# Handing a block's output to the next block by halves of the tokens, at five seams

## The reference

```python
def rmsnorm(x, g):
    xf = x.astype(jnp.float32)
    y = xf * lax.rsqrt(jnp.mean(xf * xf, axis=-1, keepdims=True) + NORM_EPS)
    return y.astype(x.dtype) * g
...
    for l in range(DEPTH):
        g = norm_gains[l]
        h = rmsnorm(x, g[0])
        ...
        x = x + rmsnorm(y, g[1])
        h = rmsnorm(x, g[2])
        x = x + rmsnorm(memory_cross_attention(h, mem_n, w_mem_q[l], w_mem_kv[l], w_mem_o[l]), g[3])
        h = rmsnorm(x, g[4])
        x = x + rmsnorm(squared_relu_mlp(h, w_ff1[l], w_ff2[l]), g[5])
```

## Time and profile before

| | us |
|---|---|
| median of 3 runs | 3533.23 |
| lowest, highest | 3530.51, 3547.64 |
| the profiled execution, its own time | 3536.43 |
| its span in the trace | 3535.1 |
| PE busy | 3241.8 (92%) |
| DVE, ACT, POOL busy | 2233.2, 1430.9, 1710.6 |

### The profile page before, as it was taken

One profiled execution on the slowest core, in us unless ns is written; L12 is line 12 of the kernel. 1 busy time (PEld: TensorE's weight loads), 2 busy tenths in 40 slices (PEclk: granted clock), 3 DMA queues, 4 the chain that ended last, 5 costly groups with the idle time before them and its releaser, 6 DMA issues.

```text
span 3535.1 us, 48085 instructions
## 1 busy us (share of the span) xinstructions
PE 3241.8 (92%) x18529; PEld 2735.6 (77%) x18529; DVE 2233.2 (63%) x3780; ACT 1430.9 (40%) x2264; POOL 1710.6 (48%) x931
## 2 busy tenths in 40 slices
PE   5997888999999888999798898999999998999997
PEld 5876676888777666888576755799999998788885
DVE  4176556555644546532567646266998995877887
ACT  4454444222434444233353424433333674333333
POOL 5742323444432313444332201447888544888884
PEclk9997999999999999999898999999999999999998
DMA  5520213444332212432221011347899898999995
GB/s 190 182 75 24 84 40 98 150 140 140 102 99 80 83 35 90 151 119 96 81 72 43 2 37 60 108 144 278 297 323 325 270 311 300 372 364 351 351 354 197
DMA packets 304819, 584.76 MB, mean 165 GB/s; under 512 B 13520, under 2 KB 224464, under 8 KB 287312
## 3 DMA queue, kind: packets, MB, share of 16 engines
q1 hardware_dynamic: 252512, 373.32, 31.2%
q0 software_dynamic: 42576, 153.83, 12.2%
q10 hardware_dynamic: 9504, 54.53, 4.0%
HBM read 522.91 MB, written 58.72 MB: 165 GB/s over the span
## 4 chain that ended last, share of the span: by engine, by line
PE 70%; DVE 9%; POOL 9%; issue 7%; ACT 4%; DMA 1%; POOLq 0%; DVEq 0%; ACTq 0%
PE bank L474 16%; PE bank L476 16%; PE bank L475 16%; POOL split_low L460 6%; PE twin L474 3%; PE twin L476 3%; PE twin L475 3%; PE bank L2858 2%; PE bank L555 2%; PE bank L2284 2%; POOL rows_arena L3224 1%; DVE branch L598 1%; PE bank L2091 1%; POOL rows_h L3224 1%; DVE residual L648 1%
## 5 line engine op out<-in xcount | busy, mean ns | idle before, releaser
L460 POOL TENSOR_TENSOR split_low<-weights,split_high 128x1024 fp32r<-128x1024 f32 x554 | 1357.1, 2456 | 1524.3 <-ACT split_high L452 1517.0
L474 PE MATMUL bank<-normed_high,split_high 128*128 128x512 f32 (+1 forms) x2032 | 751.4, 370 | 51.6 <-issue 31.0
L475 PE MATMUL bank<-normed_low,split_high 128*128 128x512 f32 (+1 forms) x2032 | 740.1, 364 | 0.0
L476 PE MATMUL bank<-normed_high,split_low 128*128 128x512 f32 (+1 forms) x2032 | 740.0, 364 | 0.0
L452 ACT CAST split_high<-weights 128x1024 fp32r<-128x1024 f32 x554 | 571.2, 1046 | 361.3 <-PE bank L476 207.1
L474 PEld LDWEIGHTS bank<-normed_high,split_high 128*128 128x128 f32 x2032 | 385.9, 190 | 101.5 <-issue 49.7
L475 PEld LDWEIGHTS bank<-normed_low,split_high 128*128 128x128 f32 x2032 | 385.9, 190 | 41.7 <-issue 2.3
L476 PEld LDWEIGHTS bank<-normed_high,split_low 128*128 128x128 f32 x2032 | 384.9, 189 | 41.5
L474 PE MATMUL bank<-split_high,wide_hidden_high 128*128 128x512 f32 x768 | 301.0, 392 | 12.6 <-DVE wide_hidden_low L3080 6.5
L475 PE MATMUL bank<-split_low,wide_hidden_high 128*128 128x512 f32 x768 | 300.0, 391 | 0.0
L476 PE MATMUL bank<-split_high,wide_hidden_low 128*128 128x512 f32 x768 | 299.8, 390 | 0.0
(11 more groups left out here) (648 smaller groups left out, 6304.3 us busy)
## 6 DMA issues: line engine op xcount, KB each, us to landing
weights<-in_w_ff SPq DMA_DIRECT2D x64, 1024.0 KB
weights<-in_peer_u SPq DMA_DIRECT2D x64, 1024.0 KB
weights<-in_peer_v SPq DMA_DIRECT2D x64, 1024.0 KB
weights<-in_cond_w SPq DMA_DIRECT2D x24, 1024.0 KB
early_table<-branch SPq DMA_DIRECT2D x128, 192.0 KB
gate_table<-arena SPq DMA_DIRECT2D x12, 2048.0 KB, 10.0
lates<-early_table ACTq DMA_DIRECT2D x32, 768.0 KB
gates<-gate_table ACTq DMA_DIRECT2D x32, 768.0 KB
```

The lines of the kernel that those rows point to most:

```text
L460: pool.do.tensor_tensor(lo, raw_unit(u), hi.bitcast(F32), ALU.subtract).then_inc(*pool.sig("split_low", u))
L474: pe.do.matmul(o, ah, bh, start=first, stop=False)
L475: pe.do.matmul(o, ah, bl, start=False, stop=False)
L476: return pe.do.matmul(o, al, bh, start=False, stop=last)
```

## The change

At each of the five seams, what is done for 512 tokens becomes twice the same for 256 tokens, and the work of the first half is put between that of the second.

- PE: where `whole_of` says 4 (the seams behind E, mem0, odd and mem1), products c = 0 to 3 stay whole, then c = 4 to 7 are made for tokens 0 to 255, then c = 4 to 7 for tokens 256 to 511. Behind mlp0 all eight go by halves. The first half's square sum stands behind the first product of the second half. Then `pe_first_halves` makes the next stage's three products for the first half of all eight operand tiles, and then for the second half.
- ACT (`act_handover`): squares, root, high operands and the next stage's weight splits in one fixed order; the first root behind the first square of the second half, and the second root behind the last square and seven (behind mlp0: six) of the first half's eight operands. The dummy Ln of `act_warm` is no longer issued at these seams.
- DVE (`dve_handover`): copies and sums, with (1, 2, 2, 0) steps of the first half's addition between them ((0, 0, 1, 0, 1, 0, 1, 0) behind mlp0).
- POOL's instructions are the same; the splits that they follow have moved on ACT: the next stage's first four units are all split during the second half's products.

The core of the diff:

```diff
+        def pe_product_halves(stage, ids, c_first, rhs, ready, emptied):
+
+            per = chunks[ids[0]].width // P
+            for t, cols_t in enumerate(HALVES):
+                for c in range(c_first, CT):
+                    ck, key = chunks[ids[c // per]], (stage, c) + half_key(t)
+                    u, cols = weights(ck, c % per)
+                    bank, empty = banks.take("product", *key)
+                    pe.wait_ge(empty, split_ready(u))
+                    for a in range(ck.n_k):
+                        pe.wait_ge(ready(a))
+                        last = triple(bank[:, 0:T // 2], [w_[:, a, cols] for w_ in unit_tiles(u)],
+                                      [r[:, cols_t] for r in rhs(a)], a == 0, a == ck.n_k - 1)
+                    last.then_inc(*pe.sig("product", *key))
+                    banks.give(("product",) + key, *emptied(c, t))
+                    used[u] = ("product",) + key
+                    yield c, t
...
+        def pe_first_halves(stage, ids, ready, emptied):
+
+            for t, cols_t in enumerate(HALVES):
+                for a in range(CT):
+                    pe.wait_ge(ready(a, t))
+                    for c in range(FIRST):
+                        u, cols = weights(chunks[ids[c // 2]], c % 2)
+                        if t == 0 and a == 0:
+                            _, empty = banks.take("product", stage, c)
+                            pe.wait_ge(empty, split_ready(u))
+                        last = triple(banks.tile("product", stage, c)[:, cols_t], [w_[:, a, cols] for w_ in unit_tiles(u)],
+                                      [r[:, cols_t] for r in h_tile(a)], a == 0, a == CT - 1)
+                        if t == 1 and a == CT - 1:
+                            last.then_inc(*pe.sig("product", stage, c))
+                            banks.give(("product", stage, c), *emptied(c))
+                            used[u] = ("product", stage, c)
...
+        def pe_close_halves(branch, halves):
+
+            for c, t in halves:
+                if t == 1 and c == whole_of(branch):
+                    pe_half_sum(branch, 0)
+            pe_half_sum(branch, 1)
+
+        def pe_half_sum(branch, t):
+            norm, key = half_post(branch, t), ("square", branch + "+") + part(branch, CT - 1, t)
+            pe_sum(norm, T // 2, 0, 2, mean, dve_tmp.tile("post_sum", branch)[:, HALVES[t]],
+                   at("post_sum", branch, *part(branch, CT - 2, t)), [("root_log", norm)])
+            pe_sum(norm, T // 2, 1, 2, mean, act_tmp.tile(*key)[:, 0:T // 2], at(*key), [("root_log", norm)])
...
+        def act_half_root(branch, t):
+            if t == 0:
+                _, empty = act_tmp.take("post_root", branch)
+                act.wait_ge(empty)
+            act_root(half_post(branch, t), 1, NORM_EPS, act_tmp.tile("post_root", branch)[:, HALVES[t]], T // 2)
+            if t == 1:
+                act_tmp.give(("post_root", branch), ("y_scaled", branch, CT - 1))
...
+        def act_handover(branch, stage, gain, ids, first):
+
+            whole = whole_of(branch)
+            for c in range(whole):
+                act_split(2 * ids[0] + c + AHEAD)
+                act_half_square(branch, c, None)
+            act_split(2 * ids[-1] + 1)
+            for c in range(whole, CT):
+                act_half_square(branch, c, 0)
+            highs = iter(range(CT))
+            for i, c in enumerate(range(whole, CT)):
+                act_half_square(branch, c, 1)
+                if i == 0:
+                    act_half_root(branch, 0)
+                if whole or i % 2:
+                    act_split(first + (i if whole else i // 2))
+                for _ in range(((1, 2, 2, 2) if whole else (0, 0, 1, 0, 1, 0, 1, 3))[i]):
+                    act_half_operand(branch, stage, gain, next(highs), 0)
+            act_half_root(branch, 1)
+            for c in highs:
+                act_half_operand(branch, stage, gain, c, 0)
             for c in range(CT):
...
+                act_half_operand(branch, stage, gain, c, 1)
...
+        def dve_half_add(branch, t, gain, x_before, stage, next_gain):
+
+            cols, r = HALVES[t], act_tmp.tile("post_root", branch)
+            for c in range(CT + 1):
+                key = half_key(t)
+                if c < CT:
+                    dve.wait_ge(at("root", half_post(branch, t)), at(*y_mark(branch, c, t)))
+                    dve.do.scalar_tensor_tensor(out=y[:, c, cols], in0=y[:, c, cols], scalar=gain(c), in1=r[:, cols],
+                                                op0=ALU.mult, op1=ALU.mult
+                                                ).then_inc(*dve.sig("y_scaled", branch, c, *key))
+                if c:
+                    b = c - 1
+                    dve.wait_ge(at("x_dve", branch, b, *key), at("operand_high", stage, b, *key))
+                    dve.do.scalar_tensor_tensor(out=h_lo[:, b, cols], in0=x[:, b, cols], scalar=next_gain(b),
+                                                in1=h_hi[:, b, cols].bitcast(F32), op0=ALU.mult, op1=ALU.subtract
+                                                ).then_inc(*dve.sig("operand_low", stage, b, *key))
+                if c < CT:
+                    dve.wait_ge(at("y_scaled", branch, c, *key), x_before(c))
+                    dve.do.tensor_tensor(x[:, c, cols], x[:, c, cols], y[:, c, cols], ALU.add
+                                         ).then_inc(*dve.sig("x_dve", branch, c, *key))
+                yield
...
+        def dve_handover(branch, gain, x_before, stage, next_gain, evacuate):
+
+            whole = whole_of(branch)
+            for c in range(whole):
+                evacuate(branch, c, None)
+                dve_half_sum(branch, c, None)
+            for c in range(whole, CT):
+                evacuate(branch, c, 0)
+                dve_half_sum(branch, c, 0)
+            early = dve_half_add(branch, 0, gain, x_before, stage, next_gain)
+            for i, c in enumerate(range(whole, CT)):
+                evacuate(branch, c, 1)
+                dve_half_sum(branch, c, 1)
+                for _ in range(((1, 2, 2, 0) if whole else (0, 0, 1, 0, 1, 0, 1, 0))[i]):
+                    next(early)
+            run(early)
+            run(dve_half_add(branch, 1, gain, x_before, stage, next_gain))
+            dve_operand_sum(stage, lambda c: y[:, c, :])
...
-            act_close(st, W["M", l, "o"])
-            act_add(st, f"mlp{l}", gain_of(l, 4), 2 * W["F", l, "up", 0][0])
+            act_handover(st, f"mlp{l}", gain_of(l, 4), W["M", l, "o"], 2 * W["F", l, "up", 0][0])
```

More of the change, by code:

```diff
@@ L697, in act_close, with whole_of @@
[L697 to L703 removed]
+        WHOLE = 4
+        def whole_of(branch):
+            return 0 if branch[:3] == "mlp" else WHOLE
@@ new lines, in act_half_square @@
+        def act_half_square(branch, c, t):
+            key = ("square", branch + "+") + part(branch, c, t)
+            cols = part_cols(branch, c, t)
+            n = cols.stop - cols.start
+            s, empty = act_tmp.take(*key)
+            if c == CT - 1 and whole_of(branch):
+                made = ("product", (branch, "o")) + part(branch, c, t)
+                tile, ready = banks.tile(*made)[:, 0:n], at(*made)
+            else:
+                tile, ready = y[:, c, cols], at(*y_mark(branch, c, t))
+            act.wait_ge(empty, ready)
+            act.do.activation(s[:, 0:n], tile, ACT.Square).then_inc(*act.sig(*key))
+            act_tmp.give(key, ("post_sum", branch) + part(branch, max(c, 1), t) if c < CT - 1
+                         else ("summed", half_post(branch, t), 1))
@@ new lines, in dve_half_sum @@
+        def dve_half_sum(branch, c, t):
+            key = part(branch, c, t)
+            if c == 0 and not t:
+                _, empty = dve_tmp.take("post_sum", branch)
+                dve.wait_ge(empty)
+            elif 0 < c < CT - 1:
+                cols = part_cols(branch, c, t)
+                n, total = cols.stop - cols.start, dve_tmp.tile("post_sum", branch)[:, cols]
+                zero = ("square", branch + "+") + part(branch, 0, t)
+                square = ("square", branch + "+") + key
+                dve.wait_ge(at(*square), at(*zero) if c == 1 else at("post_sum", branch, *part(branch, c - 1, t)))
+                dve.do.tensor_tensor(total, act_tmp.tile(*zero)[:, 0:n] if c == 1 else total,
+                                     act_tmp.tile(*square)[:, 0:n], ALU.add
+                                     ).then_inc(*dve.sig("post_sum", branch, *key))
+            elif c == CT - 1 and t == 1:
+                dve_tmp.give(("post_sum", branch), *[("summed", half_post(branch, h), 0) for h in (0, 1)])
@@ new lines, in dve_half_copy @@
+        def dve_half_copy(branch, c, t):
+            key, cols = part(branch, c, t), part_cols(branch, c, t)
+            made = ("product", (branch, "o")) + key
+            dve.wait_ge(at(*made), at("square", branch + "+", *key) if c == CT - 1 else None)
```

(5 more changed lines are left out.)

122 lines of the change are left out of this document (68 added, 54 removed).

## The result

The changed kernel is slower. Its first four runs gave a median of 3606.95 us (3599.85 to 3614.24) beside 3535.16 for the kernel before, a ratio of 1.0189 with a 95% interval of 1.0157 to 1.0221. The forecast was 3589, with a range of 3545 to 3618.

What follows compares the result with a forecast made beforehand. The seams were taken as bound by DVE and ACT making operands in turn, not PE; five seams' delays, 2 x 11.0 + 2 x 10.7 + 14.1 = 57.5, taken as 56, gave 3589 beside 3533.2, range 3545 to 3618.

Steps and rivals of the forecast that it cites:

- Steps 3 and 4: DVE's 18 half-size instructions end at 34.2 from the halved products' start; ACT's last square at 35.4; PE stands some 11.
- Three or four splits meet DVE: In each seam POOL's weight splits hold up DVE's two-input SBUF instructions by 1.2 to 2.4 each, 8.4 us together.
- Second root at 44.9: ACT reaches the second root at 41.5 from the halved products' start; with both table loads, 3.5, it ends at 44.9.
- Last low operand at 57.6 with rounds of 1.40: Behind the second root, DVE and ACT finish the second half's addition in rounds of 1.40; the seam ends at 57.6.
- +10.7 and, behind mlp0, +12.1 per seam: Growth of the stretch from the halved products' start to the last low operand: 10.7 us, or 12.1 behind mlp0.
- What follows, +2.6 in all: Sums of squares behind the seams collide with splits: +0.3 behind E and odd, nothing behind mem0 and mem1, +2 behind mlp0.
- The clock at nothing: PE's clock falls to 1.2 GHz behind the gap, but PE catches up while DVE sets the pace: priced at nothing.
- A table load costs 1.28: On ACT each table load at a root costs 1.28 us, without the Trainium skill's further drain of about 1.38.
- halves overlap: Rival, 7%: ACT squares each product at once, second root near 28, last low operand at 41; 30 us less, 3503.
- few collisions: Rival, 10%: POOL's splits slip between DVE's round trips or are granted later; 12 to 25 more in all, 3545 to 3558.
- Heavier: Rival, 5%: two more POOL splits or the clock's 2 us in each seam's path, 23 more: 3612 and above.
- The next stages have slack: Rival, 6%: the delay is made up where PE waits for splits anyway; no change or up to +17.

Runs made afterwards that it cites:

- e1: The changed kernel with no addition or operand of the first half ahead of the second root: 3589.81 us, ratio 1.0145.
- e3: The changed kernel with POOL's splits of each next stage's first four weight units cut to one element: 3568.91 us, ratio 1.0084.
- e10: The same kernel as e5, run on one chip with e9: 3600.48 us, ratio 1.0161.
- e5: The changed kernel with a dummy Ln ahead of the second half's first square and one behind the first root: 3594.84 us, ratio 1.0151.
- e9: The changed kernel again, unaltered, in five later runs: 3613.95 us, ratio 1.0196.
- e8: The changed kernel reordered: one early DVE addition step, none on ACT, Ln's table loaded before the first root, DVE's addition before the low operand: 3567.64 us, ratio 1.0077.
- e2: The changed kernel with halves only up to the second root, then addition, operands and first products whole as before: 3565.24 us, ratio 1.0087.

## Why the prediction was right, step by step

1. *First root at 18.9*: 19.0.
2. *Steps 3 and 4, the last square at 35.4 behind the early additions, PE standing some 11*: 34.9, and 5.16 + 4.57 of waiting with a mean product of 1.2 between them. The steps as summed are right, but they are not why the seam is long: in e1 the last square ends at 24.8 and the second root at 29.3, and the seam is shorter only by the collisions that fall away.
3. *Three or four splits meet DVE, 8.4 per seam*: 7.5 by e3. DVE's stretched rows are 1.54, 2.58, 2.56 and 2.60. The Trainium skill (SBUF — State Buffer, "SBUF: two separate sides") states the lock between these two engines, and e3's rows, 0.48 and 0.42 in the same places, agree.
4. *Second root at 44.9*: 44.6.
5. *Last low operand at 57.6 with rounds of 1.40*: 57.8 with 1.47. ACT's high operand is handed to DVE 0.11 after its 0.51, where I had put down 0.05, and the other pieces are a little longer too. That is 0.5 over seven rounds, and the earlier root gave 0.3 back.
6. *+10.7 and, behind mlp0, +12.1 per seam*: +10.9 and +12.2.
7. *What follows, +2.6 in all*: +3.4. The sums behind mlp0 are the +2.8 in it, forecast as +2. PE's cold mean product, 0.95 dearer behind E, I had not counted.
8. *The clock at nothing*: the step that failed in size. The seam itself is paced by DVE as I said, but the stages between took some 6 us more, 2.9 of it in mem0's, where the trace shows dips to 0.91. My 56 becomes the trace's 64.4 by 1.5 that I had taken off the sum of 57.5 because less is waited for behind mem0 and mem1, 0.9 in the seams, 0.8 behind them and 5.2 in the stages, net of the earlier start.
9. *A table load costs 1.28*: shown. Exp starts 0.01 after the load's end in the changed kernel, and e10 gained 1.0 to 1.2 per seam at the first root. By the other rule (the Trainium skill, ScalarE: Activation LUTs, "What ACT_TABLE_LOAD costs", 1.38 of drain with each) the first root would have come up to 2.66 earlier; no gap of that kind is in the rows. The median of e5 and e10 alone would have misled me.

The 18 us between the forecast and the first median are then 8 from the trace's sum and some 10 from runs: the same changed kernel fell at 3600 in two runs and between 3609 and 3618 in seven. e9's 3614 is 25 above the forecast and 4 inside the range. The rivals *halves overlap* and *few collisions* are out by e8 and by the rows. *Halves overlap* was said to turn on one point, a second root before 34.2; e1 has it at 29.3 and still ends at 53.9, so that wasn't the point. *Heavier* set its mark at 3612, which the first median doesn't reach and e9's does, but not by its mechanism, since e9's seams are those of the first execution (57.8 and 60.1); its 4.6 a seam priced the two splits, not the clock. *The next stages have slack* is out because 55.8 of the seams arrive whole at the end.

What stays open is why the clock dips where it does; I can show that both executions of the changed kernel have the dip in mem0's stage and that e1, e2 and e3 don't, not what decides it.

## What to carry to other kernels

Before a handover is cut in two, count the instructions that hand over: eight rounds of 2.21 became sixteen of 1.47, and the fixed part of each small instruction and each wait between two engines is paid twice. The overlap has to be bought from an engine that has time while the other half runs. Here the chain that sets the end is DVE's and ACT's own handing to and fro: putting its first rounds under the second half's products (the changed kernel) or behind the last copy (e1) gives the same end but for collisions, and an earlier root alone moves nothing. Move GpSimd's two-input work away from stretches in which VectorE adds, since each 2.5 us split stops one DVE instruction.

## What the runs showed of the hardware that I had not expected

One kernel's end varies from run to run. From mlp1's closing Exp to the end, work that no experiment touches, the changed kernel took 1772.5 in its first profiled execution and 1786.1 in e9's; over all twelve profiled executions of this text it lies between 1771.3 and 1786.1. PE's windows of 100 us there, first of the changed kernel, then of e9:

```profile
1927.07:2027.07 100.00, 81.88 (x1255) 0.90 0.08 28
2027.07:2127.07 100.00, 88.39 (x1699) 0.95 0.02 6
```

```profile
1931.06:2031.06 100.00, 82.90 (x1228) 0.88 0.09 32
2031.06:2131.06 100.00, 86.57 (x1595) 0.86 0.01 2
```

The granted clock is 0.86 instead of 0.95 in one such window, with a hundred matmuls fewer in it. A difference of 10 us between two kernels here is read from the stretch that was changed, not from the medians.
